# PEER gates of the second layer: one fp32 product of two fp32 one-hots per token in place of two fp16 products of three

## The chip, the cores and the metric

The kernel runs on one core of one Trainium2 chip. The metric is the device time of one execution in microseconds (us); the time of the kernel before is the median of three runs. The compute engines are TensorE (PE; its weight loads are listed as PEld), VectorE (DVE), ScalarE (ACT) and GpSimd (POOL); SP only issues DMAs. PE, DVE, ACT, POOL and SP each run their own list of instructions in order and wait for one another by semaphores.

## The reference, cut to what matters

The program is a two-layer diffusion block over 256 context and 512 latent tokens of width 1024. Each layer has a mixer and then a PEER feed-forward of 16,384 experts. Only the second PEER's gates change. What PEER computes:

```python
def peer_ffn(h, wq, k1, k2, u, v):
    q = (ht @ wq).reshape(n_tok, PEER_HEADS, PEER_QDIM)        # 8 heads
    s1 = einsum('thd,kd->thk', q[..., :PEER_HALF], k1)         # 128 first keys
    s2 = einsum('thd,kd->thk', q[..., PEER_HALF:], k2)         # 128 second keys
    t1, i1 = lax.top_k(s1, 16); t2, i2 = lax.top_k(s2, 16)
    cand_s = t1[..., :, None] + t2[..., None, :]
    cand_i = i1[..., :, None] * PEER_NK + i2[..., None, :]
    top_s, pos = lax.top_k(cand_s, 16)                         # 16 experts a head
    idx = jnp.take_along_axis(cand_i, pos, axis=-1)
    g = jax.nn.softmax(top_s, axis=-1)
    # per token: sum over its 128 choices of g * gelu(h . u[idx]) * v[idx]
```

So a token has 8 x 16 = 128 choices, each an expert (first key, second key) and a share g. Layer 1, the second and last, runs PEER over the 512 latent tokens only (4 tiles of 128 tokens).

## The kernel before, in words

The kernel gathers no experts. It computes the activation of every expert for every token, writes for each token a 128 x 128 matrix of gates (zero but for the chosen experts), and multiplies the two. `peer` (L1768) calls, one after the other, `peer_scores`, `choose_and_activate`, `combine_experts` and `project_and_norm`. The change works in `choose_and_activate` (L1080) of layer 1, in which two kinds of work run side by side.

**Activations.** 128 chunks of 128 experts. For a chunk, SP loads the expert rows `ur` (L1192), ACT casts them to fp16 `uh` (L1243), POOL computes the rest `ul = ur - uh` (L1201), PE runs 24 matmuls of 128x512 (three fp16 products over 8 blocks of the width, L1212), and ACT takes the gelu (L1250) and issues the store to `acts` (L1252). Two buffers alternate at each stage.

**Gates.** Per tile of 128 tokens, DVE picks the choices (`choices`: top 16 of each score row, L1302 to L1355), signals `chosen`, PE transposes the result (`choose`, L1221, three transposes into `T`, which lies in `G[0]`), and DVE copies it out (`cols`, L1366). The share is split for fp16 (high part L1369, rest L1370). Then come 16 gate steps of B = 8 tokens. In a step DVE copies the step's columns (`cur`, L1378) and builds for each token three one-hots over 128 lanes: the second key (L1381), the first key times the share's high part (L1382), the first key times its rest (L1383). PE multiplies (L1230): the product of `hot[.., 1, ..]` and `hot[.., 0, ..]` plus the product of `hot[.., 2, ..]` and `hot[.., 0, ..]` gives the token's gate matrix. ACT copies 8 of them into `stage` (L1266). Four stores of `stage` to `gates` (L1273) per tile are issued by ACT later.

**The order** is written out by hand in `schedule` (L1148), the same for PE and ACT. With `ahead = 12` and `beside = 8`, for each tile PE runs 12 chunks, then `choose(n)`, then 16 times one chunk and one gate step. After the last gate step come 16 more chunks (the tail). ACT follows: cast of the next chunk, gelu, store, and in the gate steps the copy of `stage`; at the start of a tile's gates it also loads the next tile's scores (`load_scores`, L1256), between the 6th and 7th of the 12 chunks it takes the exponentials (L1260) and the stores of `gates` stand around and in that part. DVE runs `choices(0)`, then `gates_of(n)`, `choices(n+1)`. Two buffers of one-hots `hot[j]` alternate: DVE may fill one for step e once the product of step e-2 is done (`prod`), and PE starts the product of step e once its one-hots stand (`hot_done`). So DVE can be two steps ahead at most. The core of it:

```python
def gate_step(n, k, e):                      # PE, L1224
    pe.wait_ge(hot_done, n * STEPS + k * E + (e + 3))
    pe.wait_ge(read, n * STEPS + k * E + (e + 1))
    for x in range(B):
        for part in (1, 2):                  # L1229, L1230
            last = nc.tensor.matmul(G[j][:, x, :], hot[j][:, x, part, :], hot[j][:, x, 0, :],
                                    start=(part == 1), stop=(part == 2))
```

Layer 0 runs the same function over 6 tiles, with `ahead, beside = 8, 6`.

Of the kernel before, what the change touches and what calls it, by code (L numbers as in the profile page):

```python
# [13 lines left out]
F32 = mybir.dt.float32  # L14
# [7 lines left out]
P = 128  # L22
# [796 lines left out]
def project_and_norm(nc, io, mods, H, src, w_name, tiles, layer, which, tag, after=None, out=None):  # L819
# [6 lines left out]
    if after:  # L826
        hh, hl, ident, next_layer, shift = after
# [4 lines left out]
    with ExitStack() as c:  # L832
# [12 lines left out]
        with signals(nc, "mvec_in", "shifting", "modulated", "turned", "high_done", "low_done", "vec_in", "prod", "read", "var_done", "rooted", "eps_set", "scaled", "normed", "own", "pown", "stored",  # L845
                     *[f"w_in{k}" for k in range(nk)]) as (
                mvec_in, shifting, modulated, turned, high_done, low_done, vec_in, prod, read, var_done, rooted, eps_set, scaled, normed, own, pown, stored, *w_in):
            with nc.Block() as block:  # L848
# [21 lines left out]
                @block.tensor  # L870
                def _(pe):
                    def product(i):
                        if i >= 2:
                            pe.wait_ge(read, i - 1)
                        for k in range(nk):
                            if i == 0:
                                pe.wait_ge(w_in[k], 16)
                            for h in range(2):
                                last = nc.tensor.matmul(ps[i % 2][:, h * 512:h * 512 + 512], src[:, k, i * P:i * P + P],
                                                        w[:, k, h * 512:h * 512 + 512], start=(k == 0), stop=(k == nk - 1))  # L880
                        last.then_inc(prod, 1)

                    def turn(i):
                        pe.wait_ge(modulated, i + 1)
                        if i >= 2:
                            pe.wait_ge(low_done, i - 1)
                        for k in range(KD):
                            last = nc.tensor.transpose(pt[i % 2][:, k, :], tmp[i % 2][:, k * P:k * P + P], ident[:, :])
# [23 lines left out]
                def _(dve):  # L912
# [31 lines left out]
                    def modulate(i):  # L944

                        t = tiles[i]
                        v = 1 if t < CTX_TILES else 0
                        dve.wait_ge(normed, i + 1)
                        if i >= 2:
                            dve.wait_ge(turned, i - 1)  # L950
                        nc.vector.scalar_tensor_tensor(tmp[i % 2][:, :], mvec[:, 2 * v + 1, :], 1.0, H[:, t, :],
                                                       ALU.add, ALU.mult).then_inc(shifting, 1)
                        dve.wait_ge(shifting, i + 1)
                        nc.vector.tensor_tensor(tmp[i % 2][:, :], tmp[i % 2][:, :], mvec[:, 2 * v, :], ALU.add).then_inc(modulated, 1)
# [125 lines left out]
def choose_and_activate(nc, io, ident, hh, hl, scores, gates, acts, layer, first_tile):  # L1080
# [10 lines left out]
    NT = TOK - c0  # L1091
# [7 lines left out]
    ahead, beside = (8, 6) if nt == TILES else (12, 8)  # L1099
# [4 lines left out]
    with ExitStack() as c:  # L1104
# [11 lines left out]
        tif = sb("tif", [P, PH, 2, PTOP])  # L1116
# [5 lines left out]
        pick = sb("pick", [P, PH, PTOP])  # L1122
# [4 lines left out]
        sel = sb("sel", [P, 3, PH, PTOP])  # L1127
        iota32 = sb("iota32", [P, P])
        iota = sb("iota", [P, P], F16)
# [11 lines left out]
        with signals(nc, *names) as (  # L1141
# [6 lines left out]
            def schedule(eng, chunk, begin, midway, choose, step_of, store):  # L1148

                def gates_of(n):
                    with eng.Fori(0, TURNS) as k:
                        done = 0
                        for e in range(E):
                            while done * E < beside * (e + 1):
                                chunk(n * (CT // 2) + k * (beside // 2) + (ahead // 2 + done // 2), done % 2)
                                done += 1
                            step_of(n, k, e)

                def choices_of(n, last):
# [12 lines left out]
                choices_of(0, None)  # L1174
                with eng.Fori(0, nt - 1) as n:
                    begin(n)
                    gates_of(n)
                    choices_of(n + 1, n)
                gates_of(nt - 1)
                for x in range(tail):  # L1180
                    if x % 2 == 0 and x // 2 < PARTS:
                        store(nt - 1, x // 2)
                    chunk((CT * nt + x) // 2, x % 2)

            with nc.Block() as block:
# [18 lines left out]
                def _(pe):  # L1204
# [19 lines left out]
                    def gate_step(n, k, e):  # L1224
# [63 lines left out]
                def _(dve):  # L1288
# [26 lines left out]
                    def choices(n):  # L1315
# [8 lines left out]
                        step.mark(nc.vector.tensor_scalar(tif[:, :, 0, :], ti[:, :, 0, :], float(PK), None, ALU.mult))  # L1324
                        step(nc.vector.tensor_copy(tif[:, :, 1, :], ti[:, :, 1, :]))
                        at = 0
                        for a0, a1, nb in RECTS:
                            shape = [P, PH, a1 - a0, nb]
                            grid = lambda x: x[:, :, at:at + (a1 - a0) * nb].rearrange("p h (a b) -> p h a b", b=nb)
                            first = lambda x: x[:, :, 0, a0:a1].unsqueeze(3).broadcast_to(shape)  # L1330
                            second = lambda x: x[:, :, 1, 0:nb].unsqueeze(2).broadcast_to(shape)
                            step.mark(nc.vector.tensor_tensor(grid(cand), first(top), second(top), ALU.add))
                            step.mark(nc.vector.tensor_tensor(grid(ci), first(tif), second(tif), ALU.add))
# [14 lines left out]
                        step(nc.vector.tensor_copy(whole[:, 0, :, :], pick[:, :, :]))  # L1348
# [6 lines left out]
                        step(nc.vector.tensor_tensor(sel[:, 2, :, :], ex[:, :, :], sm[:, :, 1:2].broadcast_to([P, PH, PTOP]), ALU.mult))  # L1355
# [8 lines left out]
                    def gates_of(n):  # L1364
                        dve.wait_ge(turned, n + 1)
                        nc.vector.tensor_copy(cols[:, 0:3, :], T).then_inc(cols_done, 1)  # L1366
                        dve.wait_ge(cols_done, n * 2 + 1)
                        gstep.base, gstep.n = n * (STEPS + 1) + 1, 0
                        gstep(nc.vector.tensor_copy(high[:, :], cols[:, 2, :]))  # L1369
                        nc.vector.tensor_tensor(cols[:, 3, :], cols[:, 2, :], high[:, :], ALU.subtract).then_inc(cols_done, 1)  # L1370
                        with dve.Fori(0, TURNS) as k:
                            gstep.base, gstep.n = n * (STEPS + 1) + k * E + 2, 0
                            for e in range(E):
                                j = e % 2
                                dve.wait_ge(prod, n * STEPS + k * E + (e + 1))
                                if e == 0:
                                    dve.wait_ge(cols_done, n * 2 + 2)
# [12 lines left out]
                    gates_of(nt - 1)  # L1390

# [5 lines left out]
def combine_experts(nc, io, gates, acts, ACC, layer, first_tile):  # L1397
# [10 lines left out]
    with ExitStack() as c:  # L1408
# [10 lines left out]
        with signals(nc, *names) as sems:  # L1419
# [4 lines left out]
            with nc.Block() as block:  # L1424
# [49 lines left out]
                def _(dve):  # L1474
# [31 lines left out]
                    add(NG - 1, 1)  # L1506

# [260 lines left out]
def peer(nc, io, mods, dram, H, hh, hl, ident, layer, first_tile, after=None, out=None):  # L1768
# [3 lines left out]
    choose_and_activate(nc, io, ident, hh, hl, scores, gates, acts, layer, first_tile)  # L1772
    with nc.sbuf_tensor(f"ACC{layer}", [P, TILES, D], F32) as ACC:
        combine_experts(nc, io, gates, acts, ACC, layer, first_tile)
# [3 lines left out]
def build(nc, io, out):  # L1778
    with ExitStack() as c:
        sb = lambda n, s: c.enter_context(nc.sbuf_tensor(n, s, F32))  # L1780
        H = sb("H", [P, TILES, D])
        ident = sb("ident", [P, P])
# [10 lines left out]
        with nc.sbuf_tensor("MIX", [P, KD, TOK], F32) as MIX:  # L1793
# [5 lines left out]
            project_and_norm(nc, io, mods, H, MIX, "ev_w_out", list(range(TILES)), 0, 0, "n0", (hh, hl, ident, 0, 3))  # L1799
        peer(nc, io, mods, dram, H, hh, hl, ident, 0, 0, (hh, hl, ident, 1, 0))  # L1800
        with nc.sbuf_tensor("MIX1", [P, RG_N, SEQ], F32) as MIX:
# [3 lines left out]
            project_and_norm(nc, io, mods, H, MIX, "od_w_out", list(range(CTX_TILES, TILES)), 1, 0, "n1", (hh, hl, ident, 1, 3))  # L1805
        peer(nc, io, mods, dram, H, hh, hl, ident, 1, CTX_TILES, out=out)


def more_inputs(give, a, k_major, swap):
# [32 lines left out]
    give("peer_v", a["peer_v"].reshape(DEPTH, PCH, P, D))  # L1842
    w = a["od_w_in"][0].reshape(KD, P, 2, RG_N, P)
# [48 lines left out]
```

## Time and profile before

| what | value |
|---|---|
| median of 3 runs | 5614.88 us (5611.41 to 5615.35) |
| the profiled execution, its own time | 5615.74 us |
| its span, first to last instruction | 5613.7 us |
| PE busy over the span | 4837.8 us (86%) |
| DVE busy | 3739.4 us (67%) |
| ACT, POOL busy | 1489.8 us (27%), 1623.5 us (29%) |
| mean granted clock of TensorE | 0.926 of full |
| `choose_and_activate` of layer 1 | about 4022 to 4881 us of the span |

A busy share is an average over stages with different limits, so the part that the change touches is read by itself below, in stretches counted in us from the start of the span. The granted clock is a share of 2.4 GHz: 1.00 is 2.4 GHz, 0.50 is 1.2 GHz. Matmuls are pipelined: a row's time of one matmul holds the end of its pipeline, so the cost of a run of matmuls is read from start to start. An fp32 matmul of the program stands in the trace as two records.

### The profile page before, as it was taken

The numbers are of one execution on the slowest core, as the hardware profiler recorded it, in microseconds if no ns is written. First come the engines' busy times: TensorE is split into PE (matmuls) and PEld (weight loads), VectorE is DVE, ScalarE is ACT, GpSimd is POOL, SyncE is SP. The second block draws the span as 40 slices with busy tenths as digits, with TensorE's granted clock in tenths as the row PEclk, the third lists the DMA queues.
The fourth block names the chain that finished last, engine by engine and source line by source line (L and its number), as shares of the span: only waits on it lengthen the run. The fifth ranks groups of instructions, "written<-read, shape, count | busy, mean of one in ns | idle before, by whom it ended". The sixth has DMA issues, their size and how long they took to land. (4 is left out here: it accounts for less than half of the span.)

```text
span 5613.7 us, 78770 instructions
## 1 busy us (share of the span) xinstructions
PE 4837.8 (86%) x25386; PEld 2519.7 (45%) x25386; DVE 3739.4 (67%) x10884; ACT 1489.8 (27%) x1771; POOL 1623.5 (29%) x700
## 2 busy tenths in 40 slices
PE   9687754789999999989999994676888898799996
PEld 1244443456566555634444442333444444344443
DVE  0213334429999999567777776683399999288886
ACT  0002222013333333322222220461233333332331
POOL 0220000432222222233333332322433333344543
PEclk9898776899999999999999997887999999999998
DMA  8210001133544455454444440102335544655553
GB/s 353 90 31 10 5 2 54 39 98 114 169 152 138 149 166 164 151 204 170 166 172 164 175 161 30 62 33 84 127 122 185 173 149 152 215 210 197 199 202 120
DMA packets 395790, 751.57 MB, mean 134 GB/s; under 512 B 26436, under 2 KB 211588, under 8 KB 391428
## 3 DMA queue, kind: packets, MB, share of 16 engines
q1 hardware_dynamic: 170792, 556.03, 27.9%
q10 hardware_dynamic: 224864, 194.07, 10.9%
q8 instruction: 46, 0.75, 0.1%
q14 instruction: 88, 0.72, 0.0%
HBM read 569.55 MB, written 180.45 MB: 134 GB/s over the span
## 5 line engine op out<-in xcount | busy, mean ns | idle before, releaser
L1469 PE MATMUL ex_R<-ex_vh,ex_wh 128*128 128x512 f16 x2560 | 972.4, 380 | 52.0 <-DVE ex_wl L1484 52.0
L1212 PE MATMUL ca_A<-hh,ca_uh 128*128 128x512 f16 (+1 forms) x3072 | 902.8, 349 | 116.4 <-POOL ca_ul L1201 116.1
L1201 POOL TENSOR_TENSOR ca_ul<-ca_ur,ca_uh 128x1024 f16<-128x1024 f32 x256 | 546.7, 2135 | 1484.8 <-ACT ca_uh L1243 1484.8
L1469 PE MATMUL ex_R<-ex_vl,ex_wh 128*128 128x512 f16 x2560 | 972.1, 380 | 0.0
L1469 PE MATMUL ex_R<-ex_vh,ex_wl 128*128 128x512 f16 x2560 | 972.0, 380 | 0.0
L1444 POOL TENSOR_TENSOR ex_vl<-ex_vr,ex_vh 128x1024 f16<-128x1024 f32 x256 | 662.1, 2614 | 989.2 <-ACT ex_vh L1453 989.2
L1212 PE MATMUL ca_A<-hl,ca_uh 128*128 128x512 f16 (+1 forms) x3072 | 901.3, 348 | 0.0
L1212 PE MATMUL ca_A<-hh,ca_ul 128*128 128x512 f16 (+1 forms) x3072 | 899.6, 347 | 0.0
L1492 DVE TENSOR_TENSOR ACC<-ACC,ex_R 128x512 f32<-128x512 f32 x640 | 408.5, 679 | 405.5 <-PE ex_R L1469 405.5
L1480 DVE TENSOR_TENSOR ex_ar<-ex_ar,ex_gr 128x768 f32<-128x768 f32 (+1 forms) x256 | 492.6, 1981 | 189.9 <-DMA ex_ar<-acts 189.2
L1453 ACT ACTIVATE ex_vh<-ex_vr 128x1024 f16<-128x1024 f32 x256 | 267.5, 1045 | 1042.9 <-PE ex_R L1469 998.9
L1382 DVE TENSOR_SCALAR ca_hot<-ca_iota,ca_cur 128x128 f16<-128x128 f16 x1280 | 527.8, 412 | 0.0
L1212 PEld LDWEIGHTS ca_A<-hh,ca_uh 128*128 128x128 f16 x3072 | 299.9, 99 | 372.0 <-ACT ca_ga L1250 74.0
L1383 DVE TENSOR_SCALAR ca_hot<-ca_iota,ca_cur 128x128 f16<-128x128 f16 x1280 | 442.9, 346 | 0.0
L1250 ACT ACTIVATE ca_ga<-ca_A 128x768 f32<-128x768 f32 (+1 forms) x256 | 180.1, 704 | 962.4 <-PE ca_A L1212 962.0
L1212 PEld LDWEIGHTS ca_A<-hh,ca_ul 128*128 128x128 f16 x3072 | 303.9, 99 | 261.6 <-issue 13.3
L1212 PEld LDWEIGHTS ca_A<-hl,ca_uh 128*128 128x128 f16 x3072 | 304.0, 99 | 249.2 <-issue 11.9
L1469 PEld LDWEIGHTS ex_R<-ex_vh,ex_wh 128*128 128x128 f16 x2560 | 250.9, 98 | 355.7 <-issue 54.8
L1469 PEld LDWEIGHTS ex_R<-ex_vh,ex_wl 128*128 128x128 f16 x2560 | 250.9, 98 | 303.4 <-issue 2.4
L1469 PEld LDWEIGHTS ex_R<-ex_vl,ex_wh 128*128 128x128 f16 x2560 | 250.9, 98 | 302.9 <-issue 1.9
L1381 DVE TENSOR_SCALAR ca_hot<-ca_iota,ca_cur 128x128 f16<-128x128 f16 x1280 | 373.6, 292 | 5.9 <-DVE ca_cur L1378 0.3
L1484 DVE TENSOR_TENSOR ex_wl<-ex_ar,ex_wh 128x768 f16<-128x768 f32 (+1 forms) x256 | 376.7, 1529 | 0.0
(305 smaller groups left out, 5978.9 us busy)
## 6 DMA issues: line engine op xcount, KB each, us to landing
ca_ur<-in_peer_u SPq DMA_DIRECT2D x256, 512.0 KB, 3.5
ex_vr<-in_peer_v SPq DMA_DIRECT2D x256, 512.0 KB, 6.9
gates<-ca_stage ACTq DMA_DIRECT2D x40, 2048.0 KB, 10.5
mod_w<-in_mod_w SPq DMA_DIRECT2D x12, 4096.0 KB, 12.4
acts<-ca_ga ACTq DMA_DIRECT2D x128, 384.0 KB, 2.3
ex_gr<-gates SPq DMA_DIRECT2D x128, 384.0 KB, 7.0
ex_ar<-acts SPq DMA_DIRECT2D x128, 384.0 KB, 7.6
acts<-ca_ga ACTq DMA_DIRECT2D x128, 256.0 KB, 2.8
```

The lines of the kernel that those rows point to most:

```text
L1201: nc.gpsimd.tensor_tensor(ul[j][:, :, :], ur[j][:, :, :], uh[j][:, :, :], ALU.subtract).then_inc(u_cut, 1)
L1212: last = nc.tensor.matmul(A[b][:, a:a + w], lhs[b][:, k, :], rhs[:, k, a:a + w], start=(k == 0 and x == 0), stop=(k == KD - 1 and x == 2))
L1250: nc.scalar.activation(ga[b][:, :], A[b][:, 0:NT], ACT.Gelu).then_inc(gelu_done, 1)
L1381: nc.vector.tensor_scalar(hot[j][:, x, 0, :], iota[:, :], w(0), None, ALU.is_equal)
L1382: nc.vector.tensor_scalar(hot[j][:, x, 1, :], iota[:, :], w(1), w(2), ALU.is_equal, ALU.mult)
L1383: last = nc.vector.tensor_scalar(hot[j][:, x, 2, :], iota[:, :], w(1), w(3), ALU.is_equal, ALU.mult)
L1444: nc.gpsimd.tensor_tensor(vl[q][:, x, :], vr[x][:, :], vh[q][:, x, :], ALU.subtract).then_inc(v_cut, 1)
L1453: nc.scalar.activation(vh[q][:, x, :], vr[x][:, :], ACT.Copy).then_inc(v_high, 1)
L1469: last = nc.tensor.matmul(R[(NP * q + y) % BANKS][:, :], lhs[q][:, x, o:o + P], rhs[q][:, x, h * 512:h * 512 + 512], start=(x == 0 and n = ...
L1480: nc.vector.tensor_tensor(ar[x][:, :], ar[x][:, :], gr[x][:, :], ALU.mult).then_inc(weighed, 1)
L1484: nc.vector.tensor_tensor(wl[q][:, x, :], ar[x][:, :], wh[q][:, x, :], ALU.subtract).then_inc(w_cut, 1)
L1492: nc.vector.tensor_tensor(part, part, R[(NP * q + y) % BANKS][:, :], ALU.add).then_inc(added, 1)
```

## The change

The diff cut to what runs. `peer` is now called with `sparse = False` in both layers and with `full = False` in layer 0, `full = True` in layer 1.

```diff
     c0 = first_tile * P
-    NT = TOK - c0
+    NT = TOK - c0 - (P if sparse else 0)
...
-    ahead, beside = (8, 6) if nt == TILES else (12, 8)
+    ahead, beside = {6: (8, 6), 5: (12, 6), 4: (12, 8), 3: (20, 10)}[nt]
...
-        tif = sb("tif", [P, PH, 2, PTOP])
+        tif = sb("tif", [P, 2, PH, PTOP])
+        pick = tif[:, 0, :, :]
...
-        pick = sb("pick", [P, PH, PTOP])
...
-        cols = sb("cols", [P, 4, P])
+        PARTS_OF = 2 if full else 3
+        cols = sb("cols", [P, PARTS_OF + 1, P])
...
-        cur = [sb(f"cur{j}", [P, 4, B]) for j in range(2)]
-        hot = [sb(f"hot{j}", [P, B, 3, P], F16) for j in range(2)]
+        cur = [sb(f"cur{j}", [P, PARTS_OF + 1, B]) for j in range(2)]
+        hot = [sb(f"hot{j}", [P, B, PARTS_OF, P], F32 if full else F16) for j in range(2)]
...
                         for x in range(B):
-                            for part in (1, 2):
+                            for part in range(1, PARTS_OF):
                                 last = nc.tensor.matmul(G[j][:, x, :], hot[j][:, x, part, :], hot[j][:, x, 0, :],
-                                                        start=(part == 1), stop=(part == 2))
+                                                        start=(part == 1), stop=(part == PARTS_OF - 1))
...
                         nc.vector.tensor_copy(cols[:, 0:3, :], T).then_inc(cols_done, 1)
-                        dve.wait_ge(cols_done, n * 2 + 1)
-                        gstep.base, gstep.n = n * (STEPS + 1) + 1, 0
-                        gstep(nc.vector.tensor_copy(high[:, :], cols[:, 2, :]))
-                        nc.vector.tensor_tensor(cols[:, 3, :], cols[:, 2, :], high[:, :], ALU.subtract).then_inc(cols_done, 1)
+                        if not full:
+                            dve.wait_ge(cols_done, n * 2 + 1)
+                            gstep.base, gstep.n = n * (STEPS + 1) + 1, 0
+                            gstep(nc.vector.tensor_copy(high[:, :], cols[:, 2, :]))
+                            nc.vector.tensor_tensor(cols[:, 3, :], cols[:, 2, :], high[:, :], ALU.subtract).then_inc(cols_done, 1)
...
                                     w = lambda row: cur[j][:, row, x:x + 1]
-                                    nc.vector.tensor_scalar(hot[j][:, x, 0, :], iota[:, :], w(0), None, ALU.is_equal)
-                                    nc.vector.tensor_scalar(hot[j][:, x, 1, :], iota[:, :], w(1), w(2), ALU.is_equal, ALU.mult)
-                                    last = nc.vector.tensor_scalar(hot[j][:, x, 2, :], iota[:, :], w(1), w(3), ALU.is_equal, ALU.mult)
+                                    row = iota32 if full else iota
+                                    nc.vector.tensor_scalar(hot[j][:, x, 0, :], row[:, :], w(0), None, ALU.is_equal)
+                                    last = nc.vector.tensor_scalar(hot[j][:, x, 1, :], row[:, :], w(1), w(2), ALU.is_equal, ALU.mult)
+                                    if not full:
+                                        last = nc.vector.tensor_scalar(hot[j][:, x, 2, :], row[:, :], w(1), w(3), ALU.is_equal, ALU.mult)
```

Three things ride along in both layers. The rows of `tif` lie in another order and `pick` takes the place of its first half (`ci` has been computed by then). A new tile `HS` of 128 x 1024 fp32 takes the modulated rows of the last tile in `project_and_norm` (L951, L954, L888) where `tmp` took them, with the same instructions. Four more inputs of 64 MB each (the experts' rows in plain order) are given to the program; they, and a function `combine_with_gathers` that would read them, belong to the `sparse` case, which neither layer uses.

## Rows read from the trace of the kernel before

**Rows 1.** Busy time by stretch: the gates of tile 0, the choices behind them.
```profile
core 0: us, PE busy (x) PEld busy (x) DVE busy (x) ACT busy (x) POOL busy (x), PEclk, DMA share, GB/s
4103.30:4217.20 113.90, 101.45 (x645) 51.92 (x644) 112.49 (x410) 40.74 (x48) 34.09 (x16) 0.99 0.37 122
4217.20:4292.30 75.10, 64.55 (x292) 28.17 (x290) 68.85 (x471) 29.56 (x32) 25.53 (x12) 0.95 0.68 207
```
**Rows 2.** Timeline of DVE and POOL in one gate step: start us, us, engine, instruction.
```profile
4188.46 0.17 DVE L1378 COPY ca_cur<-ca_cols 128x32 f32 x1
...
4189.28 0.24 DVE L1381 TENSOR_SCALAR ca_hot<-ca_iota,ca_cur 128x128 f16<-128x128 f16 x1
4189.44 0.30 DVE L1382 TENSOR_SCALAR ca_hot<-ca_iota,ca_cur 128x128 f16<-128x128 f16 x1
4189.67 0.31 DVE L1383 TENSOR_SCALAR ca_hot<-ca_iota,ca_cur 128x128 f16<-128x128 f16 x1
4189.89 0.25 DVE L1381 TENSOR_SCALAR ca_hot<-ca_iota,ca_cur 128x128 f16<-128x128 f16 x1
...
4191.84 2.13 POOL L1201 TENSOR_TENSOR ca_ul<-ca_ur,ca_uh 128x1024 f16<-128x1024 f32 x1 [4.79 <-ACT ca_uh L1243]
4191.88 2.13 DVE L1382 TENSOR_SCALAR ca_hot<-ca_iota,ca_cur 128x128 f16<-128x128 f16 x1
```
**Rows 3.** Timeline of PE, transposes and gate products alone; in brackets idle time before, releaser.
```profile
4103.34 0.49 PE L1221 MATMUL ca_G<-ident,ca_sel 128*128 128x128 f32 x3
4112.40 1.89 PE L1230 MATMUL ca_G<-ca_hot 128*128 128x128 f16 x16 [3.39 <-DVE ca_hot L1383]
...
4216.27 1.07 PE L1230 MATMUL ca_G<-ca_hot 128*128 128x128 f16 x16 [0.67 <-DVE ca_hot L1383]
4292.28 0.49 PE L1221 MATMUL ca_G<-ident,ca_sel 128*128 128x128 f32 x3
...
4310.03 1.06 PE L1230 MATMUL ca_G<-ca_hot 128*128 128x128 f16 x16
4316.11 1.06 PE L1230 MATMUL ca_G<-ca_hot 128*128 128x128 f16 x16
...
4405.40 1.07 PE L1230 MATMUL ca_G<-ca_hot 128*128 128x128 f16 x16 [0.68 <-DVE ca_hot L1383]
...
4500.86 1.06 PE L1230 MATMUL ca_G<-ca_hot 128*128 128x128 f16 x16
...
4595.63 1.07 PE L1230 MATMUL ca_G<-ca_hot 128*128 128x128 f16 x16 [0.67 <-DVE ca_hot L1383]
...
4682.56 1.88 PE L1230 MATMUL ca_G<-ca_hot 128*128 128x128 f16 x16 [3.70 <-DVE ca_hot L1383]
...
4786.57 1.07 PE L1230 MATMUL ca_G<-ca_hot 128*128 128x128 f16 x16 [0.68 <-DVE ca_hot L1383]
```
**Rows 4.** Timeline at the start of a tile's gates: ACT and PE (tile 1), POOL (tile 3).
```profile
4300.13 1.06 ACT L1243 ACTIVATE ca_uh<-ca_ur 128x1024 f16<-128x1024 f32 x1 [7.05 <-issue]
4303.51 0.61 PE L1212 MATMUL ca_A<-hh,ca_uh 128*128 128x512 f16 x1 [2.99 <-POOL ca_ul L1201]
4687.76 2.12 POOL L1201 TENSOR_TENSOR ca_ul<-ca_ur,ca_uh 128x1024 f16<-128x1024 f32 x1 [8.86 <-ACT ca_uh L1243]
```
**Rows 5.** End of DVE's choices for tile 1 (timeline); groups by line between 4217.2 and 4292.3.
```profile
4285.29 1.82 DVE L1355 TENSOR_TENSOR ca_sel<-ca_ex,ca_sm 128x128 f32<-128x128 f32 x1
...
L1212 PE MATMUL ca_A<-hh,ca_uh 128*128 128x512 f16 x96 | 37.2, 387 | 10.6 <-POOL ca_ul L1201 10.5
```
**Rows 6.** Timeline of PE elsewhere: fp32 products of 128 columns.
```profile
3941.01 2.09 PE L1042 MATMUL sc_S<-sc_keys,sc_qT 128*128 128x128 f32 x16
3942.94 0.38 PE L1035 MATMUL sc_Q<-hh,sc_wh 128*128 128x512 f16 x1
...
841.06 0.61 PE L698 MATMUL g_SC<-g_qe,g_ke 128*128 128x128 f32 x4
841.50 0.39 PE L711 MATMUL g_O<-g_sc,V 128*128 128x128 f32 x2
```
**Rows 7.** One line of DVE elsewhere: ns min/median/max, start us, forms (256 and 512 long).
```profile
L1715 DVE TENSOR_SCALAR rg_cv<-rg_z,rg_cn x20: 411/478/543, 3542.4 to 3769.6; 128x256 f32<-128x256 f32 x10, 128x512 f32<-128x512 f32 x10
```
**Rows 8.** Groups by line over the whole span: the two instructions that write `tif`.
```profile
L1324 DVE TENSOR_SCALAR ca_tif<-ca_ti 128x128 f32<-128x128 uint32 x10 | 2.3, 227 | 0.5
L1325 DVE CAST ca_tif<-ca_ti 128x128 f32<-128x128 uint32 x10 | 2.2, 220 | 0.0
```

More of the change, by code:

```diff
@@ L826, in project_and_norm @@
     if after:
-        hh, hl, ident, next_layer, shift = after
+        hh, hl, ident, next_layer, shift, HS = after
+        rows_of = lambda i: HS if HS is not None and i == n - 1 else tmp[i % 2]
     o_gate = (layer * N_MOD + 2 + 3 * which) * D
@@ L887, in turn @@
                         for k in range(KD):
-                            last = nc.tensor.transpose(pt[i % 2][:, k, :], tmp[i % 2][:, k * P:k * P + P], ident[:, :])
+                            last = nc.tensor.transpose(pt[i % 2][:, k, :], rows_of(i)[:, k * P:k * P + P], ident[:, :])
                         last.then_inc(turned, 1)
@@ L1077, with choose_and_activate @@
 CAND = sum((a1 - a0) * nb for a0, a1, nb in RECTS)
-def choose_and_activate(nc, io, ident, hh, hl, scores, gates, acts, layer, first_tile):
+def choose_and_activate(nc, io, ident, hh, hl, scores, gates, acts, chosen_rows, chosen_gates, layer, first_tile, sparse, full):
     c0 = first_tile * P
-    NT = TOK - c0
+    NT = TOK - c0 - (P if sparse else 0)
     nt = NT // P
@@ L1178, in schedule @@
                     choices_of(n + 1, n)
+                if sparse:
+                    begin(nt - 1)
                 gates_of(nt - 1)
@@ L1183, in schedule @@
                     chunk((CT * nt + x) // 2, x % 2)
+                    if sparse and x == tail // 2:
+                        midway(nt)
             with nc.Block() as block:
@@ L1313, in best16, with choices @@
                         settle()
-                    def choices(n):
+                    def choices(n, gathered=False):
                         step.start(n, CHOICE_STEPS)
@@ L1323, in choices @@
                         dve.sem_inc(s_read, 1)
-                        step.mark(nc.vector.tensor_scalar(tif[:, :, 0, :], ti[:, :, 0, :], float(PK), None, ALU.mult))
-                        step(nc.vector.tensor_copy(tif[:, :, 1, :], ti[:, :, 1, :]))
+                        step.mark(nc.vector.tensor_scalar(tif[:, 0, :, :], ti[:, :, 0, :], float(PK), None, ALU.mult))
+                        step(nc.vector.tensor_copy(tif[:, 1, :, :], ti[:, :, 1, :]))
                         at = 0
@@ L1329, in choices @@
                             grid = lambda x: x[:, :, at:at + (a1 - a0) * nb].rearrange("p h (a b) -> p h a b", b=nb)
[L1330 to L1333, printed above, removed]
+                            first = lambda x: x[:, :, a0:a1].unsqueeze(3).broadcast_to(shape)
+                            second = lambda x: x[:, :, 0:nb].unsqueeze(2).broadcast_to(shape)
+                            step.mark(nc.vector.tensor_tensor(grid(cand), first(top[:, :, 0, :]), second(top[:, :, 1, :]), ALU.add))
+                            step.mark(nc.vector.tensor_tensor(grid(ci), first(tif[:, 0, :, :]), second(tif[:, 1, :, :]), ALU.add))
                             at += (a1 - a0) * nb
@@ L1347, in choices @@
                             step.wait()
-                        step(nc.vector.tensor_copy(whole[:, 0, :, :], pick[:, :, :]))
+                        if gathered:
+                            nc.vector.tensor_copy(chosen_rows[:, :], pick.rearrange("p h k -> p (h k)"))
+                        step(nc.vector.tensor_copy(whole[:, 0, :, :], pick))
                         step.mark(nc.vector.tensor_scalar(whole[:, 1, :, :], whole[:, 0, :, :], 7, None, ALU.logical_shift_right))
@@ L1390, in _ @@
                     gates_of(nt - 1)
+                    if sparse:
+                        choices(nt, True)
 CHOICE_STEPS = 1 + (5 * 2 * PH + 4) + 2 + (2 * 4 + 1) + (5 * PH + 4) + 1 + PH * PTOP + 4 + 3
@@ L1765, in _, with peer @@
                     loop(dve, near, far, lambda m, j: None)
-def peer(nc, io, mods, dram, H, hh, hl, ident, layer, first_tile, after=None, out=None):
+def peer(nc, io, mods, dram, H, HS, hh, hl, ident, layer, first_tile, sparse, full, after=None, out=None):
     scores, gates, acts = dram
     peer_scores(nc, io, hh, hl, scores, layer, first_tile)
-    choose_and_activate(nc, io, ident, hh, hl, scores, gates, acts, layer, first_tile)
-    with nc.sbuf_tensor(f"ACC{layer}", [P, TILES, D], F32) as ACC:
-        combine_experts(nc, io, gates, acts, ACC, layer, first_tile)
+    with ExitStack() as c:
+        chosen_rows = c.enter_context(nc.sbuf_tensor(f"chosen_rows{layer}", [P, PH * PTOP], I32)) if sparse else None
+        chosen_gates = c.enter_context(nc.sbuf_tensor(f"chosen_gates{layer}", [P, PH * PTOP], F32)) if sparse else None
+        choose_and_activate(nc, io, ident, hh, hl, scores, gates, acts, chosen_rows, chosen_gates, layer, first_tile, sparse, full)
+        ACC = c.enter_context(nc.sbuf_tensor(f"ACC{layer}", [P, TILES, D], F32))
+        if sparse:
+            combine_with_gathers(nc, io, gates, acts, chosen_rows, chosen_gates, HS, ACC, layer, first_tile)
+        else:
+            combine_experts(nc, io, gates, acts, ACC, layer, first_tile)
         project_and_norm(nc, io, mods, H, ACC, None, list(range(first_tile, TILES)), layer, 1, f"n{layer}p", after, out)
@@ L1804, in build @@
                 rglru(nc, io, hh, hl, MIX, rates)
-            project_and_norm(nc, io, mods, H, MIX, "od_w_out", list(range(CTX_TILES, TILES)), 1, 0, "n1", (hh, hl, ident, 1, 3))
-        peer(nc, io, mods, dram, H, hh, hl, ident, 1, CTX_TILES, out=out)
+            project_and_norm(nc, io, mods, H, MIX, "od_w_out", list(range(CTX_TILES, TILES)), 1, 0, "n1", (hh, hl, ident, 1, 3, HS))
+        peer(nc, io, mods, dram, H, HS, hh, hl, ident, 1, CTX_TILES, False, True, out=out)
 def more_inputs(give, a, k_major, swap):
@@ L1842, in more_inputs @@
     give("peer_v", a["peer_v"].reshape(DEPTH, PCH, P, D))
+    for layer in range(DEPTH):
+        give(f"peer_u_rows{layer}", a["peer_u"][layer])
+        give(f"peer_v_rows{layer}", a["peer_v"][layer])
     w = a["od_w_in"][0].reshape(KD, P, 2, RG_N, P)
```

210 lines of the change are left out of this document (202 added, 8 removed).

## The prediction

> **What bounds the kernel now.** The change touches the gate steps of layer 1, so I read the stage in stretches first. While the gates of tile 0 are made, DVE is busy 112.49 of 113.90 us and PE 101.45; while the next choices are made, 68.85 and 64.55 of 75.10 [rows 1]. The tiles repeat this four times (three times for the choices, whose first run stands at the stage's start). DVE looks like the bound of the gate steps, and the timelines say by how much.
>
> A gate step on DVE [rows 2]: the copy of the columns, 0.20 us to the next start, then eight tokens at 0.16 for the second-key one-hot (4189.28 to 4189.44), 0.23 and 0.22 for the two parts of the share: 0.61 a token, 4.88 in all. Once a step POOL makes `ul`, and the DVE instruction that falls on it takes 2.13 in place of 0.30 [rows 2], 1.83 more. Sum 6.91 us. On PE the step ends at 4216.27 with 0.67 idle while it waits for the one-hots [rows 3]; from the first product of tile 0 to its last 15 steps take 103.87, 6.92 each. What PE would need by itself is shown where DVE has got two steps ahead: 4310.03 to 4316.11, 6.08 us with no idle time [rows 3]. Of it the 16 fp16 matmuls take 0.90 ((1.07 - 0.22)/15 each, 0.22 being the length of one), the chunk 5.18. So a step is bound by DVE at 6.92, with PE 0.84 behind it.
>
> The choices are another matter. DVE ends them at 4287.11 [rows 5], PE comes for them at 4292.28 [rows 3]: 5.2 us of slack. That stretch is set by PE's 12 chunks (12 x 5.18 = 62.2) and by 10.5 us of waits for `ul` [rows 5], which hangs on ACT's casts, not on DVE.
>
> **The change, part by part.** Four times 16 steps.
>
> *PE.* Sixteen fp16 matmuls go, eight fp32 products come. The nearest row is the score product of layer 1: eight fp32 products of 128 columns in a row, each with a fresh 128-column stationary operand, take 1.93 us from their start to the next matmul (3941.01 to 3942.94) [rows 6]. The lower end is the pair of `g_SC`, 0.44 us for two products, thus 1.76 for eight. I take 1.93: the same number in the same row, with the same operands' shapes. In place of 0.90 that is 1.03 us more a step: PE needs 5.18 + 1.93 = 7.11 us (6.94 at the lower end). The other way to the price: a single fp16 product costs 0.90/16 = 0.056, and four such passes 0.225, 1.80 for eight. By the Trainium skill (FP8 and Floating Point Precision, TensorE Precision Notes) a true fp32 product is four passes through the array; by that alone the step would be 6.98, and the row, 7% above it, decides.
>
> *DVE.* Eight of 24 one-hots go (0.22 each, 1.8 us a step). The remaining 16 read and write fp32. No fp32 one-hot stands in the trace; an fp32 instruction of the same kind with two per-partition scalars takes 411 ns at 256 elements and 543 at 512 [rows 7], which extrapolates to 345 at 128, 40 ns over the 0.305 of now. With 0.04 more for each: 0.20 + 8 x (0.16 + 0.23 + 0.08) + 1.83 = 5.8 us. The lower end is no price at all, 5.2; the upper takes the 256-element time as it stands, 0.106 more each, 6.8. At every end DVE is under PE's 7.11. So the work taken off DVE is worth nothing beyond 6.92, and **the step turns from DVE's 6.92 to PE's 7.11**.
>
> *The start of a tile.* The cast and the subtraction (L1369, L1370) go, about 0.75 us of DVE before the first one-hots, and the first eight tokens get 1.2 shorter. In tile 0 PE has idled 3.39 us there, and its products then run 1.89 in place of 1.07 [rows 3], at about the 1.2 GHz level. Now the one-hots stand 1.9 us sooner, at 4110.5; the idle 1.5 us is, I assume, no longer followed by the lower clock (if it is, 2.2 us are lost again). In tiles 1 and 2 nothing is won: the second chunk waits for ACT, which was held 7.05 us in issuing (4300.13), so PE gets it at 4303.51 after 2.99 idle [rows 4], and the second products start at 4310.03 and 4500.86 [rows 3] as before. In tile 3 the third chunk waits for POOL until 4689.88 [rows 4], thus third product at 4695.1 at the earliest; the path by PE gives 4680.5 + 2 x 7.11 = 4694.7, so the former.
>
> *The sum.* End of the last product of each tile, after against before (last start [rows 3] plus 0.89):
> - tile 0: 4110.5 + 15 x 7.11 + 1.93 = 4219.1 against 4217.2: +1.9
> - tile 1: 4310.03 + 14 x 7.11 + 1.93 = 4411.5 against 4406.3: +5.2
> - tile 2: 4500.86 + 99.54 + 1.93 = 4602.3 against 4596.5: +5.8
> - tile 3: 4695.1 + 13 x 7.11 + 1.93 = 4789.5 against 4787.5: +2.0
>
> Together +14.9 us. Tiles 1 and 2 lose most, because before, the time lost at their start was made up: DVE stood two steps ahead and PE ran at 6.08 until it had caught up. At 7.11 nothing is made up.
>
> *What does not help.* DVE ends the last one-hots some 8 us before PE's last product and starts the choices so much sooner. Their end then lies 12 us before PE asks, not 5, and PE still runs its 12 chunks at their pace; the next late thing there is ACT's issue of stores, which is untouched. The tail of 16 chunks and `combine_experts` are untouched and move as a block.
>
> *Costed at nothing.* ACT's copy of a step's gates starts 1 us later in the step; `ul` for the chunk after next then stands about 2.8 us before it is needed. The rows of `tif` in another order: the two writes take 227 and 220 ns ten times [rows 8], and even halved that is 2 us over both layers, inside choices of which PE is the bound in layer 1. `HS` changes an address. The unread inputs may place the others elsewhere in memory; I give that 5 us either way, since no row bounds it.
>
> Against the profiled execution's 5615.74 us the sum is 5630.6; it stands 0.86 above the median, so 5629.8 there, and **I forecast 5630 us**, slower by 0.27%. A measurement of this kernel can tell about 0.2%, 11.2 us, from no change.
>
> **The rivals.**
> 1. *Cheap fp32 products.* At the `g_SC` price of 1.76 a step is 6.94. The loss shrinks by 0.17 for each of some 60 steps: +4.7 us, 5620, within 0.2%. Four passes of 0.056 give +7. For it: two rows at 0.22 a product. Against it: these are bursts of two, the row of eight says 0.24. The rule of four passes in the skill leads here too.
> 2. *Faster.* Place: the products of a step. If eight fp32 products cost what the sixteen fp16 ones cost, 0.90, PE needs 6.08 and DVE 5.8, and the tiles end 14.7, 10.4, 9.8 and 12.7 us sooner: -48, 5567. The sign turns where eight products cost 1.93 - 14.9/60 = 1.68; all fp32 rows of 128 columns lie above that [rows 6].
> 3. *Slower still.* DVE stays the bound because an fp32 one-hot costs over 0.12 us more than the fp16 one, or PE's fp32 weight loads do not hide. At 0.16 more DVE needs 7.8, +0.9 over 6.92 in 60 steps: +54, 5669. Against it [rows 7] and the eight products of [rows 6], which load a new operand each.
> 4. *The choices stretch or shrink.* Their waits on issue move with the DMAs' phase, and DVE's lead could pull something along; 5 to 15 us either way, 5602 to 5640.
>
> **How the numbers follow.** The forecast's mechanism at 1.93 has 0.55 (range by itself 5622 to 5638, of which 0.08 ends within 0.2%), rival 1 has 0.22, rival 2 0.06, rival 3 0.07, rival 4 0.10 (0.04 faster, 0.03 same, 0.03 slower). Faster 0.10, same 0.33, slower 0.57. The range goes from 5611, rival 1 with memory placement in its favour, to 5643, the forecast with the low clock kept at two tile starts, placement against it and some of rival 4; it leaves out rivals 2 and 3 and the outer part of 4.
>
> **What would show it.** In the changed kernel, steps of layer 1 from product to product 7.1 us apart, PE with no idle time before a product, and DVE idle some 1.3 us a step, waiting for PE's products; eight products in about 1.93 us; one-hots of about 0.29 and 0.35 us; the choices stretch 75 us still. Wrong if the steps are under 6.9 (price of the product), if PE still waits on one-hots in the steps (price of DVE), or if the stretches outside the gates carry the difference.

## The result, and the profile after

The changed kernel takes 5622.34 us (median of 20 runs, 5618.21 to 5630.01) against 5615.35 for the kernel before (20 runs, 5609.41 to 5620.06): 7.0 us more, a ratio of 1.0015 with a 95% interval of 1.0008 to 1.0022. It is slower, by less than the 11.2 us that were set as the bound of "no change". The forecast of 5630 is 7.7 us too high; the range of 5611 to 5643 holds the result; of the three chances, the one for "within 0.2%" (0.33) was met, not the larger one for "slower" (0.57).

The busy times by stretch, for the same stretches as in [rows 1]: the gates of tile 0 and the choices behind them.

```profile
core 0: us, PE busy (x) PEld busy (x) DVE busy (x) ACT busy (x) POOL busy (x), PEclk, DMA share, GB/s
4101.20:4214.80 113.60, 112.11 (x645) 67.66 (x644) 99.21 (x327) 40.75 (x48) 34.21 (x16) 1.00 0.36 123
4214.80:4291.80 77.00, 65.80 (x289) 28.43 (x288) 57.03 (x424) 29.56 (x32) 25.70 (x12) 0.93 0.67 202
```

In the gates PE went from 101.45 busy to 112.11 of nearly the same 113.6 us, DVE from 112.49 to 99.21. The two have changed places. Of DVE's 11.8 us less in the second stretch some 7 are its lead: part of the choices is done while PE still runs gate steps. The rest is work that got shorter: four of the instructions of these choices ran beside POOL's `ul` and took 2 us each, where before it was seven.

One step on DVE and POOL, the timeline that answers to [rows 2]:

```profile
4187.19 0.18 DVE L1391 COPY ca_cur<-ca_cols 128x24 f32 x1 [1.10 <-PE ca_G L1236]
4187.41 0.29 DVE L1395 TENSOR_SCALAR ca_hot<-ca_iota,ca_cur 128x128 f32<-128x128 f32 x1
4187.61 0.34 DVE L1396 TENSOR_SCALAR ca_hot<-ca_iota,ca_cur 128x128 f32<-128x128 f32 x1
4187.86 0.28 DVE L1395 TENSOR_SCALAR ca_hot<-ca_iota,ca_cur 128x128 f32<-128x128 f32 x1
...
4189.22 2.14 POOL L1207 TENSOR_TENSOR ca_ul<-ca_ur,ca_uh 128x1024 f16<-128x1024 f32 x1 [4.83 <-ACT ca_uh L1249]
```

The bracket of the first row is new: DVE has sat idle 1.10 us, waiting for PE's product. A token costs 0.455 us now (4187.41 to 4187.86 and its neighbours) where it was 0.61.

The gate products on PE, answering to [rows 3]:

```profile
4101.23 0.49 PE L1227 MATMUL ca_G<-ident,ca_sel 128*128 128x128 f32 x3
4108.40 2.05 PE L1236 MATMUL ca_G<-ca_hot 128*128 128x128 f32 x16 [1.49 <-DVE ca_hot L1396]
4115.46 1.95 PE L1236 MATMUL ca_G<-ca_hot 128*128 128x128 f32 x16
4122.42 1.95 PE L1236 MATMUL ca_G<-ca_hot 128*128 128x128 f32 x16
...
4212.96 1.95 PE L1236 MATMUL ca_G<-ca_hot 128*128 128x128 f32 x16
4291.84 0.49 PE L1227 MATMUL ca_G<-ident,ca_sel 128*128 128x128 f32 x3
...
4309.95 1.95 PE L1236 MATMUL ca_G<-ca_hot 128*128 128x128 f32 x16
4316.91 1.95 PE L1236 MATMUL ca_G<-ca_hot 128*128 128x128 f32 x16
```

No gate product of layer 1 waits but the first of tile 0 and the first of tile 3. The steps stand 6.96 us apart: 5.18 for the chunk and 1.79 for eight fp32 products, (1.95 - 0.27)/15 = 0.112 for each of the 16 records, so 0.223 a product.

**Where the time went.** From the transposes of a tile to the end of its last product (last start plus 0.89 before, 1.79 after), and from there to the next transposes:

| stretch | before | after | difference |
|---|---|---|---|
| until the transposes of tile 0 | 4103.34 | 4101.23 | -2.1 |
| gates, tile 0 | 113.8 | 113.5 | -0.3 |
| gates, tile 1 | 114.0 | 117.4 | +3.4 |
| gates, tile 2 | 114.0 | 118.7 | +4.7 |
| gates, tile 3 | 114.3 | 114.7 | +0.4 |
| the three stretches of choices | 228.0 | 228.0 | 0.0 |
| behind the gates, to the end | 826.2 | 825.1 | -1.2 |
| span | 5613.7 | 5618.6 | +4.9 |

The gates carry +8.2. The -3.3 outside them is of the size by which executions of one kernel differ (20 runs spread over 11 to 12 us), and is taken for that. The three stretches of choices, 228.0 in sum, differ by +2.0, -0.8 and -1.1 one by one.

Tile 2 loses 1.3 us more than tile 1 though its steps are the same. The window from its transposes to the start of its second product, before and after, and then in a kernel that comes further below (every fp16 product computed twice). The granted clock is the first of the last three numbers:

```profile
4482.54:4500.86 18.32, 13.57 (x69) 6.22 (x67) 17.41 (x66) 4.11 (x5) 4.25 (x2) 0.91 0.88 279
4484.64:4504.05 19.41, 15.40 (x68) 7.65 (x67) 15.95 (x52) 4.11 (x5) 4.24 (x2) 0.82 0.83 267
4490.41:4507.25 16.84, 12.82 (x85) 6.72 (x83) 15.93 (x59) 4.11 (x5) 4.36 (x2) 1.00 0.89 281
```

In all three the second chunk starts 11.5 to 11.7 us behind the transposes, and it takes 6.8, 7.9 and 5.2 us: the granted clock stood at 0.50 for 3.4 us in the first, for 6.8 in the second and not at all in the third. That is 1.1 us of the loss in tile 2, and it is neither DVE's nor the fp32 products' pace.

### The profile page after: what moved, and what is told of

Its sections match the earlier page's. It is cut to its first block and busy times, and to the rows that moved or that the text cites. A ratio compares the mean times of both kernels' runs of the same rounds, so it can differ in the third digit from the quotient of the medians.

```text
span 5618.6 us, 78194 instructions
## 1 busy us (share of the span) xinstructions
PE 4877.0 (87%) x25386; PEld 2583.3 (46%) x25386; DVE 3657.3 (65%) x10364; ACT 1489.6 (27%) x1771; POOL 1623.5 (29%) x700
## 5 line engine op out<-in xcount | busy, mean ns | idle before, releaser
L1395 DVE TENSOR_SCALAR ca_hot<-ca_iota,ca_cur 128x128 f16<-128x128 f16 (+1 forms) x1280 | 479.4, 374 | 5.9 <-DVE ca_cur L1391 0.3
L1396 DVE TENSOR_SCALAR ca_hot<-ca_iota,ca_cur 128x128 f16<-128x128 f16 (+1 forms) x1280 | 459.3, 359 | 0.1
L1351 DVE SCALAR_TENSOR_TENSOR ca_match<-ca_iota,ca_posf,ca_ci 128x64 f32<-128x64 f16 x1280 | 342.0, 335 | 2.8
```

What stands on the lines that cost most here:

```text
L1351: step.mark(nc.vector.scalar_tensor_tensor(match[:, k, :], iota[:, 0:CAND], posf[:, h, k:k + 1], ci[:, h, :], ALU.is_equal, ALU.mult, accu ...
L1395: nc.vector.tensor_scalar(hot[j][:, x, 0, :], row[:, :], w(0), None, ALU.is_equal)
L1396: last = nc.vector.tensor_scalar(hot[j][:, x, 1, :], row[:, :], w(1), w(2), ALU.is_equal, ALU.mult)
```

## The experiments

Each ran beside the kernel before on the same chip. Differences in us are between the medians of such a set; the ratio stands with its 95% interval.

**What rides along.** The changed kernel with the gates of layer 1 made as before.

```diff
-        peer(nc, io, mods, dram, H, HS, hh, hl, ident, 1, CTX_TILES, False, True, out=out)
+        peer(nc, io, mods, dram, H, HS, hh, hl, ident, 1, CTX_TILES, False, False, out=out)
```

> The changed kernel with the gates of layer 1 made as before (two fp16 products of three one-hots); what rides along (the tif rows, HS, the four unread inputs) stays. Theory A (the +7.0 us comes from the gate steps, which PE now bounds): 0 us against the kernel before, within 2 us, gate steps 6.92 us apart. Rival B (what rides along costs it, the gate steps nothing): +5 to +9 us.

Measured: 5616.68 against 5615.98, 0.7 us, ratio 1.0002 (0.9993 to 1.0011). The steps are 6.92 apart and PE idles 0.67 before the products again:

```profile
4205.94 1.07 PE L1236 MATMUL ca_G<-ca_hot 128*128 128x128 f16 x16 [0.67 <-DVE ca_hot L1398]
4212.86 1.07 PE L1236 MATMUL ca_G<-ca_hot 128*128 128x128 f16 x16 [0.67 <-DVE ca_hot L1398]
```

So `tif`, `HS` and the unread inputs cost nothing that can be told, at most 6 us by the interval, and B with its 5 to 9 us falls but for that edge; the gate steps, which by B cost nothing, carry +8.2 in the trace above. The long fall of the clock that the change had in tile 2 is in this run too, in tile 1 and with fp16 products: 6.8 us at 0.50, and the second product 19.3 us behind the transposes.

**PE's time without an fp32 operand.** The kernel before, with each pair of fp16 products of layer 1 computed twice.

```diff
-                            for part in (1, 2):
-                                last = nc.tensor.matmul(G[j][:, x, :], hot[j][:, x, part, :], hot[j][:, x, 0, :],
-                                                        start=(part == 1), stop=(part == 2))
+                            for turn in range(2 if layer == 1 else 1):
+                                for part in (1, 2):
+                                    last = nc.tensor.matmul(G[j][:, x, :], hot[j][:, x, part, :], hot[j][:, x, 0, :],
+                                                            start=(part == 1), stop=(part == 2))
```

> The kernel before, with each pair of fp16 products of a gate step of layer 1 computed twice into the same place: 32 fp16 matmuls a step, no fp32 operand, DVE as before. Theory A (only the time on PE counts, 16 x 0.112 = 1.79 us, whatever the type): steps go from 6.92 to 5.18 + 1.79 = 6.97 us and nothing is made up after a tile's start; without the shorter DVE work at the tile starts the loss is larger than the change's: +12 to +18 us. Rival (fp32 operands cost something by themselves): 0 to +4 us here.

Measured: 5625.92 against 5615.98, +9.9, ratio 1.0017 (1.0008 to 1.0026). Its products on PE:

```profile
4116.26 3.21 PE L1231 MATMUL ca_G<-ca_hot 128*128 128x128 f16 x32 [3.39 <-DVE ca_hot L1384]
4124.49 1.95 PE L1231 MATMUL ca_G<-ca_hot 128*128 128x128 f16 x32
4131.45 1.95 PE L1231 MATMUL ca_G<-ca_hot 128*128 128x128 f16 x32
```

32 fp16 matmuls take the 1.95 us that 16 fp32 records take, and the steps stand 6.96 apart with no wait. The rival (0 to +4) is outside what was seen. The size is under the expected +12 to +18, and the tile starts tell why. In tiles 1 and 2 PE waits 2.1 and 2.5 us for the second chunk, where it waited 3.0 and 3.2 in the kernel before, because the doubled products fill part of that time; the granted clock does not fall there (the third row of the windows above), and the second products start 16.4 and 16.8 us behind the transposes in place of 17.8 and 18.3. An fp32 product of 128 columns costs PE what four fp16 ones cost, and nothing besides.

**DVE's relief with no price on PE.** The kernel before without the low part of the share in layer 1: the rest of each share is left out of the gates.

```diff
-                            for part in (1, 2):
+                            parts = (1,) if layer == 1 else (1, 2)
+                            for part in parts:
                                 last = nc.tensor.matmul(G[j][:, x, :], hot[j][:, x, part, :], hot[j][:, x, 0, :],
-                                                        start=(part == 1), stop=(part == 2))
+                                                        start=(part == 1), stop=(part == parts[-1]))
...
-                                    nc.vector.tensor_scalar(hot[j][:, x, 1, :], iota[:, :], w(1), w(2), ALU.is_equal, ALU.mult)
-                                    last = nc.vector.tensor_scalar(hot[j][:, x, 2, :], iota[:, :], w(1), w(3), ALU.is_equal, ALU.mult)
+                                    last = nc.vector.tensor_scalar(hot[j][:, x, 1, :], iota[:, :], w(1), w(2), ALU.is_equal, ALU.mult)
+                                    if layer == 0:
+                                        last = nc.vector.tensor_scalar(hot[j][:, x, 2, :], iota[:, :], w(1), w(3), ALU.is_equal, ALU.mult)
```

> The kernel before without the low part of the share in layer 1: two fp16 one-hots and one fp16 product a token, so the rest of each share is left out. What the relief of DVE is worth if PE pays nothing for it. Theory A: PE 5.18 + 0.45 = 5.63, DVE 5.1 us a step, steps 5.63 apart, about -74 us (5541). Rival (the choices or ACT bind as soon as DVE does not): -20 us or less.

Measured: 5548.69 against 5615.98, -67.3, ratio 0.9881 (0.9866 to 0.9896), with steps 5.63 apart:

```profile
4134.27 0.61 PE L1231 MATMUL ca_G<-ca_hot 128*128 128x128 f16 x8
4139.89 0.61 PE L1231 MATMUL ca_G<-ca_hot 128*128 128x128 f16 x8
4145.52 0.61 PE L1231 MATMUL ca_G<-ca_hot 128*128 128x128 f16 x8
```

Theory A has the step right. The expected -74 is 7 us too much: the gates of the four tiles are 70.0 us shorter in the trace, the three stretches of choices 2.7 longer. So the third one-hot off DVE was worth much, as long as PE did not pay for it. In the change PE pays 0.89 us a step, and DVE's relief ends where PE takes over.

**More work on DVE in the changed kernel.** Four, then eight more fp32 one-hots a step, written where nobody reads (N is 4 or 8).

```diff
+        spare = sb("spare", [P, B, P])
...
+                                    if full and x < N:
+                                        nc.vector.tensor_scalar(spare[:, x, :], row[:, :], w(1), w(2), ALU.is_equal, ALU.mult)
                                     last = nc.vector.tensor_scalar(hot[j][:, x, 1, :], row[:, :], w(1), w(2), ALU.is_equal, ALU.mult)
```

> The changed kernel with four more fp32 one-hots a step in layer 1, written to a tile that nobody reads. DVE goes from 5.8 to 5.8 + 4 x 0.26 = 6.85 us a step, still under PE's 6.97. Theory A (PE bounds the step): steps stay 6.97 apart, +0 to +3 us against the changed kernel (7 to 10 over the kernel before). Rival (DVE still matters in the step): +1.0 us a step, +60 us.

> The changed kernel with eight more fp32 one-hots a step in layer 1: DVE 5.8 + 8 x 0.26 = 7.9 us. Theory A: DVE bounds again, steps 7.9 apart, +50 to +60 us over the changed kernel, the price of all three one-hots in fp32. Rival (DVE's work is hidden by PE or by its lead of two steps): under +10 us.

Measured, with four: 5626.44 against 5616.73, +9.7, ratio 1.0019 (1.0010 to 1.0028), 2.7 us over the change's own 7.0, with overlapping intervals. With eight: 5672.72, +56.0, ratio 1.0098 (1.0083 to 1.0114), 49 over the change. A step's first DVE row with four, then the gate products of the two, four first:

```profile
4187.33 0.18 DVE L1392 COPY ca_cur<-ca_cols 128x24 f32 x1 [0.20 <-PE ca_G L1237]
```
```profile
4185.24 1.95 PE L1237 MATMUL ca_G<-ca_hot 128*128 128x128 f32 x16
4192.20 1.95 PE L1237 MATMUL ca_G<-ca_hot 128*128 128x128 f32 x16
```
```profile
4203.28 2.05 PE L1237 MATMUL ca_G<-ca_hot 128*128 128x128 f32 x16 [0.60 <-DVE ca_hot L1399]
4211.11 2.05 PE L1237 MATMUL ca_G<-ca_hot 128*128 128x128 f32 x16 [0.59 <-DVE ca_hot L1399]
```

With four the step is still 6.96 and the added microsecond of DVE work vanishes in its idle time, which goes from 1.10 to 0.20 us a step. The 2.7 us lie at the starts of tiles 0 and 3, where the first one-hots come later and the first products run at the lower clock: from the transposes to the last product's end these tiles take 116.2 and 116.3 us against the change's 113.5 and 114.7, while tiles 1 and 2 are 0.2 and 1.1 us shorter. With eight the step is 7.83 and PE waits for the one-hots again. DVE has about 1.1 us of room in the changed kernel, no more.

**The fp32 product in layer 0 too.**

```diff
-        peer(nc, io, mods, dram, H, HS, hh, hl, ident, 0, 0, False, False, (hh, hl, ident, 1, 0, None))
+        peer(nc, io, mods, dram, H, HS, hh, hl, ident, 0, 0, False, True, (hh, hl, ident, 1, 0, None))
```

> The changed kernel with the fp32 product in layer 0 too (6 tiles, 96 steps, three quarters of a longer chunk beside each). There PE's step is about 5.85 + 0.90 = 6.75 us and DVE's about 6.5, so PE bounds already. Theory A: PE grows by 0.89 us a step, +70 to +90 us against the changed kernel. Rival (the relief of DVE is worth something in layer 0): under +30 us.

Measured: 5697.06 against 5616.73, +80.3, ratio 1.0144 (1.0128 to 1.0159), 73 over the change. In layer 0 three chunks stand beside four steps, so the distance over four steps is read. The changed kernel, then this one:

```profile
1552.87 1.95 PE L1236 MATMUL ca_G<-ca_hot 128*128 128x128 f16 x32
...
1579.85 1.95 PE L1236 MATMUL ca_G<-ca_hot 128*128 128x128 f16 x32
```
```profile
1569.52 3.74 PE L1236 MATMUL ca_G<-ca_hot 128*128 128x128 f32 x32
...
1600.07 3.74 PE L1236 MATMUL ca_G<-ca_hot 128*128 128x128 f32 x32
```

26.98 for four steps against 30.55: 0.89 us a step, PE's whole price. In steps that PE bounds before the change, nothing of it is hidden. Over 96 steps that would be 86 us, and 73 were measured; the rest hides at the start of a tile, where PE has to wait anyway. In tile 2 of layer 0 the second product starts 19.6 us behind the transposes in both kernels, though the first takes 0.89 longer in one of them.

**Some tokens of each kind.** The runs say that in layer 1 DVE bounds with fp16 (6.92 against PE's 6.08) and PE with fp32 (6.96 against DVE's 5.8). A step that makes K of its 8 tokens in fp32 and the others in fp16 lies between. The edit to the kernel before, for K of 4, 3 and 2:

```diff
+        WIDE = K if layer == 1 else 0
+        wide = [sb(f"wide{j}", [P, max(WIDE, 1), 2, P]) for j in range(2)]
...
                         for x in range(B):
+                            if x < WIDE:
+                                last = nc.tensor.matmul(G[j][:, x, :], wide[j][:, x, 1, :], wide[j][:, x, 0, :], start=True, stop=True)
+                                continue
...
+                                    if x < WIDE:
+                                        nc.vector.tensor_scalar(wide[j][:, x, 0, :], iota32[:, :], w(0), None, ALU.is_equal)
+                                        last = nc.vector.tensor_scalar(wide[j][:, x, 1, :], iota32[:, :], w(1), w(2), ALU.is_equal, ALU.mult)
+                                        continue
```

> Layer 1, of the 8 tokens of a step four are made by one fp32 product of two fp32 one-hots, four by two fp16 products of three. Theory A (a step is the longer of PE and DVE): PE 5.18 + 4 x 0.223 + 4 x 0.112 = 6.52, DVE 0.2 + 4 x 0.455 + 4 x 0.61 + 1.83 = 6.3, steps 6.52 apart, -15 to -20 us, faster than both kernels. Rival (changing between the types costs PE or DVE time): steps of 6.9 or more, 0 to +7 us.

> As the mixed kernel with four fp32 tokens a step, with three. Theory A: PE 5.18 + 3 x 0.223 + 5 x 0.112 = 6.41, DVE 0.2 + 3 x 0.455 + 5 x 0.61 + 1.83 = 6.45, the two nearly level, steps 6.45 apart, -18 to -24 us. Rival (where the two are level both wait in turns): steps over 6.6, -12 us or less.

> With two fp32 tokens a step. Theory A: PE 6.30, DVE 0.2 + 2 x 0.455 + 6 x 0.61 + 1.83 = 6.60, DVE bounds again with PE idle before the products, steps 6.60 apart, -12 to -18 us. Rival (PE's time is what counts throughout): faster than the kernel with three, -24 us or more.

| tokens in fp32 | step, us | against before, us | ratio (95%) |
|---|---|---|---|
| 0 (before) | 6.92 | 0 | 1 |
| 2 | 6.67 | -14.7 | 0.9972 (0.9963 to 0.9981) |
| 3 | 6.41 | -20.7 | 0.9966 (0.9952 to 0.9979) |
| 4 | 6.52 | -16.9 | 0.9970 (0.9959 to 0.9981) |
| 8 (the change) | 6.96 | +7.0 | 1.0015 (1.0008 to 1.0022) |

The step lengths are read from rows like these, for three tokens and then for two:

```profile
4192.07 0.83 PE L1232 MATMUL ca_G<-ca_wide 128*128 128x128 f32 x6
...
4198.48 0.83 PE L1232 MATMUL ca_G<-ca_wide 128*128 128x128 f32 x6
```
```profile
4192.04 0.71 PE L1232 MATMUL ca_G<-ca_wide 128*128 128x128 f32 x4
...
4198.71 0.71 PE L1232 MATMUL ca_G<-ca_wide 128*128 128x128 f32 x4
```

All three mixed kernels beat both kernels, and the rivals of all three runs fall. With four, the step is PE's 6.52, and DVE idles 0.04 us a step: there the two are level. With three, PE's sum (5.18 + 0.67 + 0.56 = 6.41) is met, but not because DVE keeps up: DVE has no idle time from the sixth step of a tile on and takes about 6.5 us for most steps. It starts a tile two steps ahead, and 16 steps are too few to use that up in tiles 0 to 2. In tile 3 it is used up, and the last seven steps stand 6.51 apart:

```profile
4751.89 0.94 PE L1232 MATMUL ca_G<-ca_wide 128*128 128x128 f32 x6
...
4758.40 0.93 PE L1232 MATMUL ca_G<-ca_wide 128*128 128x128 f32 x6
```

With two, the lead lasts for the first few steps of tiles 0 to 2 (three, six and eight steps of 6.3, PE's pace); from there on, and in tile 3 after the second step, the steps are DVE's 6.67. So theory A, the longer of the two, holds where the lead is gone, and PE's pace before. That three is better than two or four shows in the step lengths; the intervals of the times overlap.

## Why the prediction came out as it did

*PE takes over from DVE in the step.* Right, and shown from both sides: no idle time before the products of the steps after the change, and DVE's room measured by the added one-hots. The terms of DVE were right too: 0.455 us a token against 0.47, and one-hots of 0.28 and 0.34 us against 0.29 and 0.35.

*The price of eight fp32 products.* This is the term of the sum that was mis-sized: "I take 1.93: the same number in the same row". Measured are 1.79. The row of [rows 6] was read as eight products in one run, but it merges two groups of four. The same product in narrower windows of the timeline of the kernel before (each time the records in flight in the window), with ACT's copy between them:

```profile
3941.01 1.05 PE L1042 MATMUL sc_S<-sc_keys,sc_qT 128*128 128x128 f32 x8
...
3941.94 1.16 PE L1042 MATMUL sc_S<-sc_keys,sc_qT 128*128 128x128 f32 x8
...
3941.29 0.60 ACT L1054 ACTIVATE sc_qT<-sc_Q 128x512 f32<-128x512 f32 x1 [4.58 <-PE sc_Q L1035]
```

The first eight records are (1.05 - 0.27)/7 = 0.111 apart, so they would be over at 3941.90, and the second group's operand `qT` is ready only when ACT is, at 3941.89. The merged row, 1.93 from start to the next matmul, holds this handover, and it costs 0.14 us in two ways: the second group starts 0.04 late, and it takes 1.16 where the first takes 1.05. The gate products show the same 0.10 behind a wait: 2.05 for the first of tile 0, 1.95 for the next. Rival 1 had the price nearly right (1.76 from `g_SC`, 1.80 from four passes of 0.056), and with it the verdict "within 0.2%". That its +7 is the medians' 7.0 is in part luck, since the gates carry 8.2 in the trace. The rule of four passes in the Trainium skill (FP8 and Floating Point Precision, TensorE Precision Notes), which the prediction set below its row, agrees with the runs: 0.223 us a product is four times the 0.056 of an fp16 one, and computing fp16 pairs twice gave the same step.

*The sum.* With 1.79 in place of 1.93 the same sum gives 6.97 a step, and from transposes to last end 113.5, 117.1, 117.7 and 114.3 us for the four tiles; the trace has 113.5, 117.4, 118.7 and 114.7. Together that is +6.5 where the prediction had +14.9, the trace's gates say +8.2 and the medians +7.0. The one term is 8.4 us too high. Against the trace's gates, about 1.7 us of that were made good by an error the other way: the second products of tiles 1 and 2 and the third of tile 3 came 0.4, 1.1 and 0.4 us later than "as before" and "at the earliest" had it, tile 2's for the lower clock. In rival 2 the four tiles come to 14.6, 10.3, 9.6 and 12.5 us by its own terms, about 47 in sum and not 47.6; nothing hangs on that.

*The start of a tile.* Right: in tile 0 the products begin 7.2 us behind the transposes, not 9.1, and PE does not drop to the lower clock (2.05 for 16 records, where a run with four more one-hots has 3.54). That the clock would stay up was an assumption without a row behind it, and it held; the rows at the end of this document show how near the other outcome was. In tile 1 the second product starts 18.1 behind the transposes where it was 17.8, held by ACT's issuing as before, and the time lost there is not made up. That is why tiles 1 and 2 carry the loss, with 1.1 us in tile 2 for the lower clock, and tiles 0 and 3 almost none.

*The choices gain nothing from DVE's lead.* Right: 228.0 and 228.0 us, though DVE begins them 6 us before the last product starts. It then waits for PE's transposes even longer than the predicted 12 us:

```profile
4292.37 0.56 DVE L1375 COPY ca_cols<-ca_G 128x384 f32<-128x384 f32 x1 [19.52 <-PE ca_G L1227]
```

*Rivals 2 to 4.* Faster by cheap fp32 products: ruled out by 0.223 a product. DVE still the bound, or weight loads that do not hide: ruled out by steps of 6.96 without a wait and by the run with four more one-hots, and the first made real by the run with eight. The choices did not move in sum, and what rides along costs nothing measurable.

## What to carry to other kernels

Where two engines pace a step within 15% of each other, work shifted from one to the other gains at most the gap between them; cost both sides, and if the shift can be made for part of the items, choose the part that nearly levels the two (three of eight here, -20.7 us, where all eight cost 7.0). Count the lead too: an engine that stands two steps ahead at a loop's start may be the slower one for a while without costing anything, and the faster one makes up lost time meanwhile. Where the waiting engine becomes the bound, that reserve is gone. Before a price is taken from a merged row, look inside it for a wait: narrow the window until the starts are evenly spaced.

## What was not expected of the hardware

An fp32 product of 128 columns with a new 128-column stationary operand each time costs 0.223 us on PE, also over eight in a row: the weight loads, 0.19 us for each of the two records, hide, but for 0.10 us once behind a wait. And the granted clock at a tile's start depended on small things. Without work for 1.49 us before the first product of tile 0, PE ran the 16 records in 2.05 us, at a granted clock of 1.00 (2.4 GHz). With four more one-hots it was 2.64 us without work, and 3.54 for the records, with the clock at 0.50 (1.2 GHz) for most of them:

```profile
4114.00 3.54 PE L1237 MATMUL ca_G<-ca_hot 128*128 128x128 f32 x16 [2.64 <-DVE ca_hot L1399]
4113.80:4117.10 3.30, 3.10 (x14) 3.11 (x15) 3.27 (x16) 0.00 (x0) 0.00 (x0) 0.50 0.57 214
```

The idle time alone does not tell which it will be. With three fp32 tokens PE stood without work for 3.02 us before the first product of tile 3, and the clock stayed at 1.00:

```profile
4667.30 0.93 PE L1232 MATMUL ca_G<-ca_wide 128*128 128x128 f32 x6 [3.02 <-DVE ca_hot L1392]
4660.00:4672.00 12.00, 8.98 (x52) 4.65 (x51) 11.67 (x47) 2.24 (x3) 2.12 (x1) 1.00 0.91 265
```
